# Swapping the memory projections and alternating two 64-row score tiles in a two-block transformer kernel

## The reference

```python
x = x + 0.5 * swiglu(rms_norm(x, norm_ffn1), ffn1_w1, ffn1_w3, ffn1_w2)
x = x + hybrid_mixer(rms_norm(x, norm_mix), w_in, ...)         # retention (4 heads of 128) and
                                                               # differential attention (4 heads, 2 halves of 64)
x = x + memory_attention(rms_norm(x, norm_mem_q), rms_norm(mem, norm_mem_kv), mem_w_q, mem_w_kv, mem_w_o, ...)
x = x + 0.5 * swiglu(rms_norm(x, norm_ffn2), ...)
return rms_norm(x, norm_out)

def diff_attention(q, k, v, lam):          # q, k: (S, 4, 2, 64), causal, ALiBi
    sc = einsum('bqhmd,bkhmd->bhmqk', q_blk, k) * scale - slopes * dist
    p = softmax(sc)
    return einsum('bhqk,bkhe->bqhe', p[:, :, 0] - lam * p[:, :, 1], v)

def memory_attention(h, mem_n, w_q, w_kv, w_o, q_norm, k_norm):     # mem: 256 tokens, 4 heads of 256
    q = rms_norm(h @ w_q, q_norm); k, v = split(mem_n @ w_kv); k = rms_norm(k, k_norm)
    return softmax(q k^T / 16) v @ w_o
```

## Time and profile before

| | |
|---|---|
| median of 3 runs | 2133.57 us |
| the profiled execution: its time, its span | 2131.61 us, 2129.8 us |
| PE busy | 2081.2 us, 98% of the span |
| DVE, ACT, POOL busy | 1170.8, 865.9, 328.2 us |
| stages `diff 0` to the end of `mv` | 1285.7 to 1584.8 us |
| stage `out2` | 1584.8 to 1628.3 us |
| TensorE clock granted | 0.993 of full speed over the span |

### The profile page before, as it was taken

How to read it: one execution, slowest core, us unless ns; L and a number is a source line. 1 busy time by engine, 2 the same in 40 slices (tenths; PEclk the granted TensorE clock), 3 DMA queues, 4 the chain that set the end, 5 groups by cost and what they waited for, 6 DMA issues and landing times.

```text
span 2129.8 us, 26955 instructions
## 1 busy us (share of the span) xinstructions
PE 2081.2 (98%) x10562; PEld 1749.8 (82%) x10562; DVE 1170.8 (55%) x2216; ACT 865.9 (41%) x1644; POOL 328.2 (15%) x526
## 2 busy tenths in 40 slices
PE   8999999999999999999999999999989999999998
PEld 7777888888888888878888889878878888888887
DVE  6676546575444344674543445666755665444445
ACT  6556344354423233543322324544444443332324
POOL 2311000021000001221110113312532011110101
PEclk9999999999999999999999999999999999999999
DMA  5141432123323333223333322212242123332223
GB/s 173 53 131 60 117 84 82 60 69 99 107 93 98 99 99 99 80 84 96 98 99 99 99 87 97 70 65 90 92 137 80 60 80 99 99 99 91 94 83 129
DMA packets 197879, 198.62 MB, mean 93 GB/s; under 512 B 3820, under 2 KB 193068, under 8 KB 197676
## 3 DMA queue, kind: packets, MB, share of 16 engines
q1 hardware_dynamic: 197752, 196.89, 29.3%
HBM read 194.66 MB, written 6.93 MB: 95 GB/s over the span
## 4 chain that ended last, share of the span: by engine, by line
PE 88%; DVE 3%; POOL 3%; issue 3%; ACT 2%; DMA 0%; SPq 0%; DVEq 0%; POOLq 0%; ACTq 0%
PE ps L601 24%; PE ps L607 24%; PE ps L604 24%; PE ps L610 2%; PE ps L613 2%; PE ps L616 2%; POOL m L693 1%; PE ps L1102 1%; PE ps L1391 1%; DVE m L641 0%; ACT m L632 0%; PE ps L1859 0%; PE ps L1382 0%; POOL m L1679 0%; POOL m L819 0%
## 5 line engine op out<-in xcount | busy, mean ns | idle before, releaser
L601 PE MATMUL ps<-m,m 128*128 128x512 f32 (+1 forms) x2432 | 951.0, 391 | 2.0 <-ACT m L890 2.0
L607 PE MATMUL ps<-m,m 128*128 128x512 f32 (+1 forms) x2432 | 939.5, 386 | 0.0
L604 PE MATMUL ps<-m,m 128*128 128x512 f32 (+1 forms) x2432 | 938.9, 386 | 0.5 <-DVE m L641 0.5
L632 ACT ACTIVATE m<-m 128x512 fp32r<-128x512 f32 x688 | 400.0, 621 | 579.3 <-PE ps L607 545.8
L641 DVE TENSOR_TENSOR m<-m,m 128x512 fp32r<-128x512 f32 x688 | 512.4, 762 | 64.3 <-ACT m L632 60.7
L601 PEld LDWEIGHTS ps<-m,m 128*128 128x128 f32 x2432 | 458.1, 188 | 94.4 <-issue 5.4
L607 PEld LDWEIGHTS ps<-m,m 128*128 128x128 f32 x2432 | 457.7, 188 | 94.0 <-DVE m L912 1.2
L604 PEld LDWEIGHTS ps<-m,m 128*128 128x128 f32 x2432 | 458.3, 188 | 87.1 <-DVE m L641 0.7
L1596 POOL TENSOR_TENSOR m<-m,m 128x512 f32<-128x512 f32 x44 | 76.2, 1732 | 492.7 <-DVE m L1573 492.7
L610 PE MATMUL ps<-m,m 128*128 128x256 f32 x512 | 151.7, 296 | 0.3 <-ACT m L2194 0.3
L613 PE MATMUL ps<-m,m 128*128 128x256 f32 x512 | 146.7, 287 | 1.5 <-DVE m L641 1.4
(11 more groups left out here) (333 smaller groups left out, 1966.2 us busy)
## 6 DMA issues: line engine op xcount, KB each, us to landing
m<-ffn_w SPq DMA_DIRECT2D x60, 1024.0 KB, 5.3
m<-w_ff SPq DMA_DIRECT2D x32, 1024.0 KB, 5.4
m<-w_in SPq DMA_DIRECT2D x28, 1024.0 KB, 5.2
m<-ffn_w SPq DMA_DIRECT2D x12, 768.0 KB, 4.5
m<-w_in SPq DMA_DIRECT2D x17, 512.0 KB, 5.1
m<-w_out SPq DMA_DIRECT2D x8, 1024.0 KB, 5.2
m<-mem_w_kv SPq DMA_DIRECT2D x8, 1024.0 KB, 5.5
m<-w_out_a SPq DMA_DIRECT2D x4, 1024.0 KB, 5.1
```

The lines of the kernel that those rows point to most:

```text
L601: pe.matmul(o, lh, xh, start=k == 0, stop=False)
L604: pe.matmul(o, ll, xh, start=False, stop=False)
L607: done = pe.matmul(o, lh, xl, start=False, stop=k == nk - 1)
L632: act.activation(self.WH[b % 2][:, at], self.RAW[b % 2][:, at], ACT.Copy).then_inc(*self.up("w_hi", b, c))
```

## The change

- The blocks of `mv` stand before those of `mk` in the plan.
- `mx` is made during `ret 1` (from 1.7 blocks into it, one piece every 0.14 block) instead of in one go at the start of the memory stage, and lies in a region of its own, which later holds the finished memory keys. The raw keys `mraw` move too.
- The transposes of the four normed keys, and the splits behind them, move to places 0.02, 0.06, 0.55 and 1.05 of `out2`. Queries and memory attention wait for the last of them.
- The two halves of a differential unit become one visit: six matmuls, taken in turn from half 0 (bank 3) and half 1 (bank 7).
- Places: the transposes of the differential norm and their splits are 2 US later, differential attention 0.2 block later, retention's turn back and what follows it 0.5 block later, and the split of the first retention values 0.2 block later.

```diff
-        spare = sb(0, [P, KT, S])
-        self.mraw = [spare[:, 2 * i:2 * i + 2, 256:512] for i in range(4)]
-        self.mx = Operand([self.XGh[:, k, 0:256] for k in range(KT)], [self.XGl[:, k, 0:256] for k in range(KT)],
+        self.mraw = [pa(88 + 2 * i, [P, 2, 256])[:, :, :] for i in range(4)]
+        self.mx = Operand([pa(k, [P, 256], R32)[:, :] for k in range(KT)], [pa(8 + k, [P, 256], R32)[:, :] for k in range(KT)],
                           lambda k: self.at("mx_hi", k), lambda k: self.at("mx_lo", k))
...
         wkv = self.io["mem_w_kv_2"]
+        self.stage("mv", [Block([(wkv[:, D + 256 * j:D + 256 * j + 256], 0)], 8, 256,
+                                [Job(("mv", j), self.mx, 0, 256, j2, tiles=(0, 1))]) for j in range(4)])
         self.stage("mk", [Block([(wkv[:, 256 * h:256 * h + 256], 0)], 8, 256,
                                 [Job(("mk", h), self.mx, 0, 256, j2, tiles=(0, 1))]) for h in range(4)])
-        self.stage("mv", [Block([(wkv[:, D + 256 * j:D + 256 * j + 256], 0)], 8, 256,
-                                [Job(("mv", j), self.mx, 0, 256, j2, tiles=(0, 1))]) for j in range(4)])
...
-                  "mq": [self.filled(("mv", 3)), self.filled(("rqk", 1, 2, 1)), self.filled(("turn_mk", 3))], "f2": [self.filled(("mq", 7))]}[v]
+                  "mq": [self.filled(("rqk", 1, 2, 1))], "f2": [self.filled(("mq", 7))]}[v]
...
-        yield place + 7 * US
+        yield place + 9 * US
...
-        yield place + 8 * US
+        yield place + 10 * US
...
-        yield self.normed_place(s, n, m) + 6.5 * US
+        yield self.normed_place(s, n, m) + 8.5 * US
...
-        return self.start["diff", s] + 3.8 + 1.3 * e if s == 0 else self.start["diff", 1] + 3.9 + 1.3 * e
+        return self.start["diff", s] + 4.0 + 1.3 * e if s == 0 else self.start["diff", 1] + 4.1 + 1.3 * e
...
-        for m in range(2):
-            yield at + 0.12 * m
-            half, c, name = slice(64 * m, 64 * m + 64), slice(i * P, i * P + P), ("qk_d", k, i, m)
-            made = [self.cleared(("turn_n", self.normed_n(s, x, y))) for x in (1, 2) for y in range(2)]
-            for w in new(*made, *self.claim(name, 3)):
-                pe.wait_ge(*w)
-            out = self.bank(name)[:, 0:n]
-            pe.matmul(out, qh[half, e, c], kh[half, e, 0:n], start=True, stop=False)
-            pe.matmul(out, qh[half, e, c], kl[half, e, 0:n], start=False, stop=False)
-            pe.matmul(out, ql[half, e, c], kh[half, e, 0:n], start=False, stop=True).then_inc(*self.full(name))
+        yield at
+        c, names = slice(i * P, i * P + P), [("qk_d", k, i, m) for m in range(2)]
+        made = [self.cleared(("turn_n", self.normed_n(s, x, y))) for x in (1, 2) for y in range(2)]
+        for w in new(*made, *self.claim(names[0], 3), *self.claim(names[1], 7)):
+            pe.wait_ge(*w)
+        for step, (q, x) in enumerate(((qh, kh), (qh, kl), (ql, kh))):
+            for m in range(2):
+                half, out = slice(64 * m, 64 * m + 64), self.bank(names[m])[:, 0:n]
+                done = pe.matmul(out, q[half, e, c], x[half, e, 0:n], start=step == 0, stop=step == 2)
+                if step == 2:
+                    done.then_inc(*self.full(names[m]))
...
-            yield at + 0.1 + 0.12 * m
+            yield at + 0.1 + 0.07 * m
...
-            yield at + 0.18 + 0.12 * m
+            yield at + 0.18 + 0.08 * m
...
-        for step, src, after in ((0, None, 1.15), (1, "ret_normed", 3.1)):
+        for step, src, after in ((0, None, 1.15), (1, "ret_normed", 3.6)):
...
-            yield self.start["mk"] + 0.01 + 0.04 * k
-            for w in new(self.at("memT"), self.filled(("rqk", 1, 2, 1))):
+            yield self.start["ret", 1] + 1.7 + 0.14 * k
+            for w in new(self.at("memT"), self.filled(("pv_r", 1))):
...
-            yield self.start["mk"] + 0.03 + 0.04 * k
+            yield self.start["ret", 1] + 1.76 + 0.14 * k
...
+    def turn_mk_place(self, h):
+        return self.start["out2"] + (0.02, 0.06, 0.55, 1.05)[h]
...
-        for w in new(self.filled(("mk", h)), self.filled(("rqk", 1, 2, 1)), self.at("row_sums", "mk", h - 1) if h else self.filled(("mem_sums",))):
+        for w in new(self.filled(("mk", h)), self.filled(("pv_r", 3)), self.at("row_sums", "mk", h - 1) if h else self.filled(("mem_sums",))):
...
-        yield place + 1.45
-        for w in new(self.filled(("turn_mk", h)), self.filled(("pv_r", 1)), self.at("constants")):
+        yield self.turn_mk_place(h) + 0.1
+        for w in new(self.filled(("turn_mk", h)), self.filled(("mk", 3)), self.at("constants")):
...
-            yield place + 1.52 + 0.06 * f
+            yield self.turn_mk_place(h) + 0.17 + 0.06 * f
...
-        yield self.mk_place(h) + 1.35
+        yield self.turn_mk_place(h)
...
-            before = [self.filled(("out2", 7))]
+            before = [self.filled(("out2", 7)), self.filled(("turn_mk", 3))]
...
-            for w in new(self.filled(name), self.at("nrq_m", h), self.filled(("out2", 7)),
+            for w in new(self.filled(name), self.at("nrq_m", h), self.filled(("out2", 7)), self.filled(("turn_mk", 3)),
...
-                              [self.filled(("pv_d", 2 * i + 1))], b["ret", i] + 0.3 * m + 0.8, self.dv_parts(i, m, "rv"))
+                              [self.filled(("pv_d", 2 * i + 1))], b["ret", i] + 0.3 * m + 1.0 - 0.2 * i, self.dv_parts(i, m, "rv"))
...
```

More of the change, by code:

```diff
@@ L2118, in act_finish_r @@
         act.activation(sq, turned, ACT.Square).then_inc(*self.up("ret_sq", k))
-        yield at + 3.4
+        yield at + 3.9
         for w in new(self.cleared(("ret_turn", k, 1))):
@@ L2142, in dve_finish_r @@
         self.dve_seed(dve, new, q)
-        yield at + 3.25
+        yield at + 3.75
         g = self.SG[:, k, :]
@@ L2148, in dve_finish_r @@
                                  op1=ALU.mult).then_inc(*self.drained(("ret_turn", k, 1)))
-        yield at + 3.5
+        yield at + 4.0
         for w in new(self.at("mix_hi", k)):
@@ L2720, in vector @@
         s += [self.dve_finish_d(dve, new, k) for k in range(4)]
-        s += [self.dve_values(dve, new, ("rv", i, m), self.nm["mx2"]["r"], b["ret", i] + 0.3 * m + 0.87, self.dv_parts(i, m, "rv"))
+        s += [self.dve_values(dve, new, ("rv", i, m), self.nm["mx2"]["r"], b["ret", i] + 0.3 * m + 1.07 - 0.2 * i, self.dv_parts(i, m, "rv"))
               for i in range(2) for m in range(2)]
```

## The result

| | before | after |
|---|---|---|
| median of 4 runs each | 2133.52 us | 2106.68 us (2105.93 to 2108.3) |
| ratio, with its 95% interval | | 0.9877 [0.986, 0.9894] |
| the profiled execution: its time, its span | 2131.61, 2129.8 us | 2108.3, 2106.5 us |

The forecast was 2106.2 us, within 2100 to 2118. The medians lie 26.8 us apart, the two profiled executions 23.3: before's is 1.9 us under its median, after's 1.6 over. After lost 1.5 us ahead of the change's reach, since `diff 0` starts at 1285.7 us before and at 1287.2 after. The granted clock goes with it: from 20 to 50 us of the span it is 0.89 before and 0.83 after, 1.8 us of work lost to the lower level. From `diff 0` to the start of `out2` it is 299.1 us before and 272.4 after (-26.7); `out2` then grows by 1.9. The change is thus worth 24.8 us in this pair of traces.

A forecast was written before the change was run, and what follows sets the result against it. PE, busy 98% of 2129.8 us, was taken to bound the kernel, so gains lay in its losses. Terms 7.8 + 2.7 + 2.5 + 1.2 + 4.0 + 1.0 + 5.9 + 4.8 - 2.5 = 27.4 us off 2133.57 gave 2106.2 us, range 2100 to 2118.

The forecast's parts named there:

- waits at retention's turns (POOL, ACT): Memory stage: values before keys free POOL for retention's units 2 and 3, so waits of 6.3 and 1.5 us go.
- stretch at clock 0.50: After retention's longest wait, 5.74 us ran at the lower clock; without that wait, 2.7 us less.
- memory key's wait: With the keys' transposes moved into `out2`, PE's 2.5 us wait for a memory key goes.
- wait before retention's scores: Making `mx` in `ret 1` relieves DVE; 1.2 of the 2.2 us wait before the scores goes.
- the norm's transposes: Differential norm: transposes 2 US later remove three waits for normed queries and keys, 4.0 us.
- restart of PE: Each PE wait costs a little beyond its idle time; six removed waits of 0.16 us make 1.0 us.
- 16 fewer visits, and overlap: Differential units: 16 visits saved at 0.37 us, 5.9 us; halves partly overlapping, loads going singly, 4.8 us.
- new waits: Shifted pieces in fixed queues and visits needing two banks: one wait of the memory key's size, 2.5 us lost.
- rival 2: Differential units: full overlap, pairs of matmuls cost one, 3.0 us more gained, 2103.2 us; chance 0.11.
- Rivals 1, 4 and 5: Differential halves: no overlap, 2111.0 us, 0.18; each alternation a switch, 2125.8, 0.05; each waits for matmul end, 2139.0, 0.03.
- Rival 6: Retention: POOL's 12 operations, not their order, are too long; 4.0 + 6.3 + 2.7 us stay, 2119.2 us; chance 0.05.
- Rival 3: A POOL wait returns, likeliest at head 3's turn in `out2` (cover 3 us); 9.0 us lost, 2115.2 us; chance 0.12.

The follow-up runs named there:

- experiment 4: The changed kernel with a merged unit's six matmuls each on its own line, half 0's three before half 1's three; single time 2107.0 us.
- experiment 2: The changed kernel with the two differential halves in separate visits through bank 3 again, all other places and the memory's order as changed; 2116.66 us.
- experiment 7: The changed kernel with retention's turn back at 3.1 blocks instead of 3.6, the places behind it moved likewise; 2114.26 us.
- experiment 1: The kernel before with only the merged, alternating differential visit, its two banks and its DVE and ACT places; 2123.38 us, ratio 0.9953.
- experiment 5: The changed kernel with the differential norm's transposes and splits 2 US earlier again, differential attention left as changed; 2113.41 us.
- experiment 3: The changed kernel with half 0's three matmuls and then half 1's three in the merged visit, instead of in turn; 2108.36 us.
- experiment 6: The kernel before with only retention's turn back and what follows it 0.5 block later; 2134.88 us over ten runs, ratio 1.0007.

## Why the prediction was right, and where its steps were not

The terms of the sum against what the profiled pair and the runs show:

| term | forecast | measured |
|---|---|---|
| waits at retention's turns (POOL, ACT) | 7.8 | 7.5 (7.8 to 0.3) |
| stretch at clock 0.50 | 2.7 | 2.7 (none left) |
| memory key's wait | 2.5 | 2.5 |
| wait before retention's scores | 1.2 | 0.2 (2.2 to 1.2, and 0.8 new for L2010) |
| the norm's transposes | 4.0 | 2.3 (4.0 to 1.7) |
| restart of PE | 1.0 | not told apart |
| 16 fewer visits, and overlap | 5.9 + 4.8 | 13.6 together (13.5 by the starts) |
| new waits | -2.5 | -5.0 |
| sum | 27.4 | 24.8, with the restart taken as forecast |

The new waits are 1.5 us more at L1859 than before, 1.6 at L1894, 1.6 more at L1867 and 0.3 at L1883. The 24.8 us are what the traces lost from `diff 0` to the end of `out2`. So the account closes, but for the 1.0 us of the restart, which no run tells apart. The forecast's total stands on an error of +2.9 and several that add to -5.5; that it came within 0.6 us of the 26.8 between the medians is luck.

Two of the signs that the prediction had named failed. The waits on L2164, L1815 (after's L1814) and L2284 are 2.0 us together, not under 1, and the differential stage is 9.4 us shorter, not 14. The others held: no stretch at the lower clock from 1300 to 1600 us, no wait at a turn of `out2`, and `mk` and `mv` 15.7 us shorter. One slip of the working changes nothing: the visit's 0.95 us is one distance of 0.12, three of 0.237 and 0.12, and not "five distances of 0.12".

**The overlap was under-sized.** The step that failed is "if they go singly, a pair needs 0.22 us". I took the rhythm of loads from the earlier trace rows, where all loads go into the same 64 rows, and applied it to loads that go into different ones. Experiment 4's starts show the full 7.8 us within 0.2, and experiment 2 agrees: rival 2's term. By the Trainium skill ("TensorEngine Tiling (Array Packing)", Key Properties) different tiles load and multiply in parallel, and the traces agree: 0.01 us from load to load and from start to start. "Within 0.8 us if loads set the pace" thus didn't tell the cases apart; 0.58 us is below it, and I had named no figure for full overlap. Rivals 1, 4 and 5 are excluded by the same rows: going from one half to the other costs nothing that shows.

The page "TensorE: Matmul & The Clock Gate" of the Trainium skill (Part 3: Packing small matmuls) says of such packed matmuls that they start and end strictly in program order. Here the trace disagrees: in experiment 4 the fourth matmul starts 0.33 us ahead of the second, and the measurement decides. That each engine executes its queue strictly in order, as said ahead of the prediction, thus needs this exception for PE.

**The visits' 0.37 us stands.** The timelines of after still have 0.21 us into a unit (0.32 between matmuls of 512 columns, as in before), now 16 times, and a merged unit is as long as one visit was, to 0.01 us.

**POOL's order was the cause, but the cover was misjudged.** I wrote that unit 3's pieces "need about half of the time between their places". They are one chain with unit 2's. POOL's timeline in after:

```profile
1520.29 1.36 POOL L2159 TENSOR_TENSOR m<-m,m 128x512 f32<-128x512 f32 x1 [14.01 <-DVE m L2132]
...
1527.96 1.37 POOL L2164 TENSOR_TENSOR m<-m,m 128x512 f32<-128x512 f32 x1
1529.29 1.49 POOL L2159 TENSOR_TENSOR m<-m,m 128x512 f32<-128x512 f32 x1
1532.93 0.20 POOL L818 TENSOR_TENSOR m<-m 128x4 f32<-128x4 f32 x1 [2.15 <-DVE m L789]
...
1537.91 1.36 POOL L2164 TENSOR_TENSOR m<-m,m 128x512 f32<-128x512 f32 x1
```

Unit 3's mean starts the moment unit 2's scaling is done, and its own scaling ends at 1539.27. PE's turn is reached 0.3 us earlier. From the start of the mean to the end of the scaling it is 10.0 us, of which 2.15 are a wait for DVE, where the prediction had put 1.04 + 1.04 + 3.4. The earlier trace rows already had it: 1547.49 to 1558.08, 10.6 us. The cover isn't half the time, it is gone; the 0.5 block of the later place is all that holds the wait at 0.3 us, as experiment 7 shows. This was luck in the forecast: by its own step the new order alone would have been enough. Rival 6 (the pieces, not their order, are too long) had the right doubt for the order taken by itself.

**DVE was the blind spot.** "New waits: one of the memory key's size" stood for 2.5 us, and 5.0 came, all of it on DVE. That a shorter unit leaves every piece behind it less time follows from the forecast's own gain: 10.7 us taken out of 16 units are 0.67 us from each. I priced the places that the change moves and not those that it leaves where they are while the time under them shrinks. Experiment 1 has it pure: of 3.5 us more waits from the shorter unit alone, 2.9 are for DVE, and experiment 5 shows it at the norm, where the old places would cost 6.7 us now. The differential stage was therefore 9.4 us shorter, not 14.

**Rival 3 didn't happen.** Head 3's turn in `out2` has no wait; PE is busy all 45.40 us of that stage. But the cover was 1.2 us and not 3: POOL's scaling for it ends at 1571.40 us, and PE turns at 1572.59.

## What to carry to other kernels

Matmuls on the two halves of the rows ran side by side at all four sizes measured here, loads included, and the order in the program need not even alternate; what costs is going into and out of the 64-row mode (0.37 us a visit), so gather such matmuls into one visit with a PSUM bank for each half. A queue in fixed order hands a wait on: before moving one customer's place, follow the whole chain on the engine it waits for, because the wait may only change its name. And when matmul time goes out of a unit, list the pieces of the other engines that keep their places, for each of them has lost as much time.

## What the hardware did that I had not expected

- Matmuls on different halves of the rows don't keep the program's order among themselves: the fourth starts 0.01 us behind the first and 0.33 us ahead of the second (experiment 4), and running them in a row instead of in turn changes the time by 1.7 us, inside the intervals (experiment 3).
- Such a pair costs the time of one, to 0.01 us a unit, at 128, 256, 384 and 512 columns (experiment 4).
- How long a stretch at clock 0.50 is, and whether there is one, doesn't follow from the wait alone. It was 3.4 us at waits of 1.94 and 2.87 us (experiment 5), of 2.91 us (experiment 6) and of 4.60 us (experiment 7), and 6.8 us at the wait of 7.01 us (experiment 6). The wait of 2.50 us for a memory key in experiment 1 brought none, nor did after's waits, of which the longest is 1.7 us.
